# A decoder layer on one core: the mixing stage normalises one unit ahead, 18 of 48 expert tiles are turned in the projection, and the first branch weights are loaded before their stage

## What is computed

```python
h = rmsnorm(x, g_norm1) * (1.0 + scale1) + shift1
aq, ak, av, bb, bc, bx, cz, dq, dk, dv, gl = jnp.split(h @ w_in, SPLIT_POINTS, axis=-1)
ya = diff_attention(aq, ak, av, ...)                 # 4 heads, causal, softmax of two score maps each
yb = short_conv_mixer(bb, bc, bx, conv_w)
yc = multiscale_pool(cz, w_pool, pool_scale)
yd = sliding_window_sink_attention(dq, dk, dv, sinks) # 8 heads on 2 key heads, window of 128
branches = jnp.einsum('bsgc,gcd->bsgd', jnp.stack([ya, yb, yc, yd], axis=2), w_branch)
gates = jax.nn.sigmoid(gl.reshape(Bn, S, N_BRANCH, D_MODEL))
x = x + gate1 * (jnp.sum(gates * branches, axis=2) @ w_o)
return x + gate2 * peer_ffn(rmsnorm(x, g_norm2) * (1.0 + scale2) + shift2, ...)
```

## Time and profile before

| | us |
|---|---|
| median of 3 runs (lowest, highest) | 2081.24 (2071.46, 2083.84) |
| the profiled execution | 2083.53 |
| its span in the profile | 2081.7 |
| TensorE busy in the span | 1884.9 (91%) |
| VectorE, GpSimd, ScalarE busy | 1490.5, 770.8, 721.6 |

### The profile page before, as it was taken

The page is one execution under the profiler, slowest core; times in us unless marked ns, Lnnn a source line. Parts: engine busy times, 40 slices in busy tenths (PEclk is TensorE's granted clock), DMA queues, the critical chain, the costliest instruction groups (busy, mean ns, idle before and its releaser), DMA issues. The chain is left out here.

```text
span 2081.7 us, 28455 instructions
## 1 busy us (share of the span) xinstructions
PE 1884.9 (91%) x10096; PEld 1643.4 (79%) x10096; DVE 1490.5 (72%) x2260; ACT 721.6 (35%) x969; POOL 770.8 (37%) x487
## 2 busy tenths in 40 slices
PE   4999888889698989998999998999869999999998
PEld 4888666667486978888998988898858888888886
DVE  6444366665355658899987588878848888887887
ACT  3222233343324221323332354555533333333331
POOL 0000194000024000457877777787732332333320
PEclk7999989999799989999999999999989999999999
DMA  8754188888876051459999989999999999999991
GB/s 286 263 182 141 46 231 244 240 237 244 279 222 198 15 124 41 104 151 247 278 267 250 294 227 308 318 324 323 320 335 379 386 383 368 363 353 356 365 351 71
DMA packets 325795, 526.33 MB, mean 253 GB/s; under 512 B 20266, under 2 KB 243291, under 8 KB 321116
## 3 DMA queue, kind: packets, MB, share of 16 engines
q1 hardware_dynamic: 288860, 391.23, 61.6%
q0 software_dynamic: 36864, 134.23, 18.9%
HBM read 438.88 MB, written 85.99 MB: 252 GB/s over the span
## 5 line engine op out<-in xcount | busy, mean ns | idle before, releaser
L119 PE MATMUL u_s<-h_hi,u_hi 128*128 128x384 f32 x1024 | 359.2, 351 | 51.1 <-POOL u_lo L1775 46.4
L121 PE MATMUL u_s<-h_hi,u_lo 128*128 128x384 f32 x1024 | 350.0, 342 | 0.0
L120 PE MATMUL u_s<-h_lo,u_hi 128*128 128x384 f32 x1024 | 349.7, 342 | 0.0
L119 PE MATMUL v_o<-v_v_hi,v_w_hi 128*128 128x512 f32 x768 | 300.0, 391 | 19.1 <-DVE v_w_lo L1998 18.2
L120 PE MATMUL v_o<-v_v_lo,v_w_hi 128*128 128x512 f32 x768 | 299.6, 390 | 0.0
L121 PE MATMUL v_o<-v_v_hi,v_w_lo 128*128 128x512 f32 x768 | 299.5, 390 | 0.0
L119 PEld LDWEIGHTS u_s<-h_hi,u_hi 128*128 128x128 f32 x1024 | 197.9, 193 | 64.5 <-POOL u_lo L1775 38.0
L1937 ACT ACTIVATE v_v_hi<-v_raw 128x1024 fp32r<-128x1024 f32 x128 | 127.6, 1051 | 340.4 <-PE v_o L121 275.9
L1775 POOL TENSOR_TENSOR u_lo<-u_ut,u_hi 128x1024 fp32r<-128x1024 f32 x79 | 196.3, 2486 | 94.8 <-ACT u_hi L1553 94.4
L1964 DVE TENSOR_TENSOR v_v_lo<-v_raw,v_v_hi 128x1024 fp32r<-128x1024 f32 x128 | 149.4, 1220 | 92.7 <-ACT v_v_hi L1937 92.4
L120 PEld LDWEIGHTS u_s<-h_lo,u_hi 128*128 128x128 f32 x1024 | 198.0, 193 | 0.0
(11 more groups left out here) (310 smaller groups left out, 3879.1 us busy)
## 6 DMA issues: line engine op xcount, KB each, us to landing
v_raw<-in_v_experts_dram SPq DMA_DIRECT2D x128, 512.0 KB, 5.7
u_raw<-in_u_experts_dram SPq DMA_DIRECT2D x160, 256.0 KB, 6.3
gate_w_u_raw<-in_u_experts_dram SPq DMA_DIRECT2D x192, 128.0 KB, 4.0
turned_experts<-gate_w_u_t SPq DMA_DIRECT2D x48, 512.0 KB, 4.1
expert_acts<-u_ao SPq DMA_DIRECT2D x64, 384.0 KB, 5.3
u_raw<-turned_experts SPq DMA_DIRECT2D x96, 256.0 KB, 11.5
expert_gates<-u_gs SPq DMA_DIRECT2D x12, 2048.0 KB, 11.9
v_gt<-expert_gates SPq DMA_DIRECT2D x32, 768.0 KB, 14.4
```

Source lines behind the costliest of these rows:

```text
L119: nc.tensor.matmul(out, w[0], x[0], start=first, stop=False)
L120: nc.tensor.matmul(out, w[0], x[1], start=False, stop=False)
L121: return nc.tensor.matmul(out, w[1], x[0], start=False, stop=last)
```

## The change

Three things are done.

1. In `phase_mix` VectorE normalises unit n+1 in iteration n, after its scores were taken an iteration earlier, then turns rows, then does the split, then the scores of unit n+2. ScalarE does the exponentials of unit n+2 behind the split and ahead of the tanh. SyncE loads gate weights behind the turned rows and ahead of its wait for the tanh. In the last eight products the turn also stands ahead of the split.
2. 18 of the 48 tiles are turned in `phase_project`, between blocks 1 and 12, three in two blocks; the loops of SyncE, ScalarE and VectorE are written out there. The buffers lie where the results of blocks 13 to 16 go, so ScalarE waits for the turned tiles to be stored before it writes block 13. The other 30 are turned in the first 28 steps of `phase_mix` (`TURNING`), about one in each.
3. After step 28 of the mixing stage SyncE waits until all turned tiles are stored and loads the first two weight blocks of the gate stage into the two buffers of the turned tiles. The gate stage takes them from there, and its own buffers can take blocks 2 and 3 at once. VectorE waits for its second split before it writes over them.

```diff
-AHEAD = NE // P - PLAIN
+GATED = NE // P - PLAIN
+FRONT = 0
+AHEAD = GATED + FRONT
+IN_PROJECT = 18
+IN_MIX = AHEAD - IN_PROJECT
...
+def turned_tile(n):
+    return PLAIN + n if n < GATED else n - GATED
...
+FIRST_TURN, LAST_TURN = 1, 12
+def projected_by(b):
+    return IN_PROJECT * max(0, min(LAST_TURN, b) + 1 - FIRST_TURN) // (LAST_TURN + 1 - FIRST_TURN)
...
+            rows_in(0)
+            rows_in(1)
+            for b in range(4, NB):
+                i, j = b // 4, b % 4
                 sp.wait_ge(lo_ok, b - 3)
                 sp.dma_start(raw[j][:, :, :], cols(b)).then_inc(w_in[j], 16)
-            with sp.Fori(1, NB // 4) as i:
-                for j in range(4):
-                    load(4 * i + j, j)
-                    if j >= 2:
-                        sp.wait_ge(share_ok, 16 * i + 8 * (j - 1) - 16)
-                        sp.dma_start(ring[j - 2][:, :, :], ada[:, :, bass.ds((4 + 2 * i + j - 2) * S, S)]).then_inc(ada_in[j - 2], 16)
-            load(NB - 1, 0)
+                if i < 4 and j >= 2:
+                    sp.wait_ge(share_ok, 16 * i + 8 * (j - 1) - 16)
+                    sp.dma_start(ring[j - 2][:, :, :], ada[:, :, (4 + 2 * i + j - 2) * S:(5 + 2 * i + j - 2) * S]).then_inc(ada_in[j - 2], 16)
+                for t in range(projected_by(b - 4), projected_by(b - 3)):
+                    sp.wait_ge(u_turned, t + 1)
+                    sp.dma_start(turned_slot(turned, t), u_t[t % 2][:, :, :].rearrange("p m e -> p (m e)")).then_inc(u_out[t % 2], 16)
+                    if t + 2 < IN_PROJECT:
+                        rows_in(t + 2)
+            for j in range(2):
+                sp.wait_ge(u_out[j], 16 * (IN_PROJECT // 2))
...
+                if b == LAST_TURN + 1:
+                    act.wait_ge(u_turned, IN_PROJECT)
+                    for x in range(2):
+                        act.wait_ge(u_out[x], 16 * (IN_PROJECT // 2))
...
+            def turn_rows(b):
+                for t in range(projected_by(b - 1), projected_by(b)):
+                    j = t % 2
+                    dve.wait_ge(u_in[j], 64 * (t // 2) + 64)
+                    if t >= 2:
+                        dve.wait_ge(u_out[j], 16 * (t // 2))
+                    turn_tile(nc, u_t[j], u_raw[j]).then_inc(u_turned, 1)
...
+                turn_rows(4 * i)
                 split_lo(4 * i + 2, 2)
                 shares(i, range(5, 11))
+                turn_rows(4 * i + 1)
                 split_lo(4 * i + 3, 3)
                 shares(i, range(11, 16))
+                turn_rows(4 * i + 2)
...
+TURNING = 28
 def turned_by(n):
-    return AHEAD * (n + 1) // (NBR * KD)
-def phase_mix(nc, a, keep, xt, y_hi, y_lo, tanhs, turned):
+    return IN_MIX * min(n + 1, TURNING) // TURNING
...
+            sp.wait_ge(sem["g_lo"], 1)
+            load(2)
             for n in range(NG):
-                if n + 2 < NG:
-                    sp.wait_ge(sem["g_lo"], n + 1)
-                    load(n + 2)
                 for t in range(turned_by(n - 1), turned_by(n)):
                     sp.wait_ge(sem["u_turned"], t + 1)
-                    sp.dma_start(turned[t // 2, :, t % 2 * D:(t % 2 + 1) * D], u_t[t % 2][:, :, :].rearrange("p m e -> p (m e)")).then_inc(sem[f"u_out{t % 2}"], 16)
-                    if t + 2 < AHEAD:
+                    sp.dma_start(turned_slot(turned, IN_PROJECT + t), u_t[t % 2][:, :, :].rearrange("p m e -> p (m e)")).then_inc(sem[f"u_out{t % 2}"], 16)
+                    if t + 2 < IN_MIX:
                         rows_in(t + 2)
+                if n + 3 < NG:
+                    sp.wait_ge(sem["g_lo"], n + 2)
+                    load(n + 3)
+                if n == TURNING:
+                    for j in range(2):
+                        sp.wait_ge(sem[f"u_out{j}"], 16 * (IN_MIX // 2))
+                        load_branch(sp, a, b_first[j], 1, j).then_inc(first_in[j], 16)
                 sp.wait_ge(sem["th_ok"], n + 1)
                 sp.dma_start(tanhs[n], th[n % 2][:, :]).then_inc(sem[f"th_out{n % 2}"], 16)
...
             exps(0)
+            exps(1)
             for n, (kind, i, h) in enumerate(units):
-                if n + 1 < NU:
-                    exps(n + 1)
                 act.wait_ge(sem["tr"], n + 1)
                 if n >= 2:
                     act.wait_ge(sem["pv"], n - 1)
                 nb = len(blocks(n))
                 nc.scalar.activation(pt[:, n % 2, 0:nb, :], p_t[:, 0:nb, :], ACT.Copy).then_inc(sem["pt_ok"], 1)
                 split_hi(n + 1)
+                if n + 2 < NU:
+                    exps(n + 2)
                 tanh(n)
...
             scores_in(0)
             split_lo(0)
+            scores_in(1)
+            normalise(0)
             for n in range(NU):
                 if n + 1 < NU:
-                    scores_in(n + 1)
-                normalise(n)
+                    normalise(n + 1)
+                turn_rows(n)
                 split_lo(n + 1)
-                turn_rows(n)
+                if n + 2 < NU:
+                    scores_in(n + 2)
...
+def load_branch(eng, a, to, g, d):
+    wb = a["w_branch"][0].rearrange("g (k p) n -> p (g k) n", p=P)
+    return eng.dma_start(to[:, :, :], wb[:, CB * g:CB * g + CB, d * BW:(d + 1) * BW])
...
+                if not isinstance(r, int) or r:
                     sp.wait_ge(sem["lo_ok"], s - 1)
-                sp.dma_start(raw[j][:, :, :], wb[:, bass.ds(4 * g, CB), d * BW:(d + 1) * BW]).then_inc(sem[f"b_in{j}"], 16)
+                if not isinstance(r, int) or r or d >= 2:
+                    sp.dma_start(raw[j][:, :, :], wb[:, bass.ds(4 * g, CB), d * BW:(d + 1) * BW]).then_inc(sem[f"b_in{j}"], 16)
...
+                first = isinstance(r, int) and s < 2
+                if first:
+                    act.wait_ge(first_in[j], 16)
+                else:
+                    act.wait_ge(sem[f"b_in{j}"], (2 * r + d // 2) * 16)
                 if wait:
                     act.wait_ge(sem["mm"], 2 * s - 2)
-                nc.scalar.activation(hi[j][:, :, :], raw[j][:, :, :], ACT.Copy).then_inc(sem["hi_ok"], 1)
+                nc.scalar.activation(hi[j][:, :, :], (b_first if first else raw)[j][:, :, :], ACT.Copy).then_inc(sem["hi_ok"], 1)
...
+                    if first and d == 1:
+                        dve.wait_ge(sem["lo_ok"], 2)
```

More of the change, by code:

```diff
@@ L456, in _ @@
             turn(0, True)
-            with dve.Fori(1, NB // 4) as i:
+            for i in range(1, NB // 4):
                 turn(i)
@@ L2078, in program @@
         tanhs = nc.dram_tensor("gate_tanhs", [NBR * KD, P, S], F32, kind="Internal").ap()
[L2079 to L2080 removed]
+        kb = Kit(nc, top, "branch", Y_AT + 56 * KB)
+        b_first, first_in = [kb.sb(f"first{j}", [P, CB, BW]) for j in range(2)], [kb.sem(f"first_in{j}") for j in range(2)]
+        phase_mix(nc, a, keep, xt, *(y[:, :, :].rearrange("p (g c) t -> p g c t", c=CB) for y in (y_hi, y_lo)), tanhs, turned, b_first, first_in)
         if stop <= 3:
```

68 lines of the change are left out of this document (36 added, 32 removed).

## The result

The changed kernel takes 2025.56 us (median of 4 runs, 2024.32 to 2035.27), the kernel before 2081.7 us beside it (4 runs, 2071.46 to 2083.84). The ratio is 0.9746, 95% interval 0.9707 to 0.9785. The forecast was 2036 us, range 2018 to 2056. The profiled execution took 2025.17 us, with a span of 2023.3.

What follows compares the result with a forecast made beforehand. The prediction took the mixing stage to be held by an order of hand-overs, no engine but TensorE being full. Its terms, -31 - 8.3 - 8.6 + 3 = -45 us, took the median 2081.2 to 2036 us, range 2018 to 2056.

Steps and rivals of the forecast that it cites:

- The units, -31: Mixing stage's 24 attention units: normalising one unit ahead removes waits for normalised scores; 202 us, 31 us less.
- The 9 us for GpSimd's company: First ten attention units: GpSimd working beside VectorE lengthens the loop by 0.9 us each, 9 us.
- the thin place: ScalarE's queue in the units: tanh behind the next exponentials, expected done some 1.5 us before TensorE needs it.
- The eight products, -8.3: Last eight gate products of the mixing stage: earlier weight requests, no turns after unit 27; 58.8 becomes 50.5 us.
- The gap, -8.6: Before the first branch product: last tanh store issued earlier and weights already loaded, so it starts 8.6 us earlier.
- The projection, +3: First 13 projection blocks: 18 added turns bring transfers near their limit; cost between 0 and 11 us, 3 taken.
- After 570 us, nothing: Rest of the kernel: the change touches only the gate stage's first loads there, so no saving was counted.
- B: Rival: VectorE, ScalarE and GpSimd's lock-outs make the loop bind; units 216 us, total 2050; chance 0.14.
- C: Rival: TensorE hardly waits; units 191 us, tail 49, nothing lost in the projection, total 2020; chance 0.12.
- D: Rival: in the units the wait only moves to the tanh; tail and gap alone gain, total 2067; chance 0.05.
- A: The forecast case itself, all terms as summed: 2036 us (2027 to 2047); chance 0.65.
- E: Rival: turns in the projection pace its blocks through transfers, 15.6 us instead of 10.9 each; total 2090; chance 0.04.

Runs made afterwards that it cites:

- the repeats: Two more groups of runs of the changed kernel with nothing edited: medians 2028.46 and 2029.85 us.
- light_pool: The changed kernel with GpSimd leaving out the pooling's adds and two of three convolution taps, so the output differs: 2022.35 us.
- late_pool: The changed kernel with GpSimd's pooling and convolution held back until unit 11 has ended: 2031.33 us.
- tanh_first: The changed kernel with ScalarE taking the tanh of product n before the exponentials of unit n+2: 2025.31 us.
- after_again: The changed kernel run once more with nothing edited: 2028.46 us, ratio 0.9766 to the kernel before.
- all_in_mix: The changed kernel with no tiles turned in the projection, all 48 in the mixing stage by unit 27: 2056.87 us.
- old_order: The changed kernel with VectorE's and ScalarE's steps in the order of the kernel before, the other parts kept: 2045.31 us.
- turn_24: The changed kernel with 24 tiles turned in the projection instead of 18, and 24 in the mixing stage: 2034.69 us.
- z_split: The changed kernel with GpSimd's 128x2048 product of the convolution's inputs issued as four of 128x512: 2026.93 us.
- after: The changed kernel itself, as first measured and profiled: 2025.56 us, ratio 0.9746 to the kernel before.

## Why the prediction was right

**The units, -31.** Measured -31.7, and -30.2 and -29.7 by the repeats. The waits for normalised scores went whole (39.0 to 7.0: the 32 I took). TensorE's busy time fell by 10.6 us, where I took 8 for the clock. That this is close is in part luck: I had matmuls in 16 of the 28 us at 1.2 GHz and let all of those go, while they were in 27.7 and 17.4 of these went, and the clock explains 8.7 us, not all of the 10.6. The 9 us for GpSimd's company came as 10.7 us of waits for the tanh, 8.6 of it at products 3 and 9 and not spread over ten units; the two small waits come behind 390 us, where GpSimd is silent. That GpSimd's company is the cause light_pool and late_pool confirm; its price in late_pool, 11.3 us, is near the 9. The step behind it, that the tanh queued behind the exponentials is the thin place, holds: tanh_first takes the waits away. In the wide units, where loop and cycle had come out equal, TensorE hardly waits: it is busy 113.93 of the last 116.10 us (after_again, above).

**The eight products, -8.3.** Measured -8.6. The number was right and its reason only in part. I put it down to the weights' earlier request and to turns that end with unit 27. all_in_mix has both and takes 57.4 us, 1.1 less than the kernel before. The rest came with the lower number of tiles (five turned in these products and not seven, at a share of 0.67 and not 0.81 for the transfers), which I counted for the loop of the units alone; old_order, with the same five tiles and the old order, takes 51.1.

**The gap, -8.6.** Measured -9.9. The issue of the last store, 0.8 us after the transposes began, and the 2.37 us from the split to TensorE came as I said. Mis-sized were the store's landing (2.46 us, not 3.48) and the 0.3 us from there to the split (0.03). The prediction cites the Trainium skill (DMA: Bandwidth & Descriptors, Anatomy of one DMA) for a fixed cost of about 2.0 us. That section is on transfers that GpSimd issues, and this store is SyncE's; no run here splits its 2.46 us.

**The projection, +3.** Measured 0: TensorE was busy 141.66 of 141.90 us. The sum of demand (144 to 153 us of transfers in 142) was about right, a share of 0.98, but I charged a wait where the last transfers simply ran on beside blocks that turn nothing. How near the edge it is, turn_24 shows: 7 us for six tiles more.

**After 570 us, nothing.** The profile after had 8.2 us less there, 7.3 of it in the gathered phase. The prediction rightly gave the change nothing; what it lacked was the spread of that phase, 18 us over fourteen profiles, one per cent of the span less a little. With it the error resolves: the parts up to the first branch product sum to -50.2 us, where -45 was forecast (3 from the projection, 1.3 from the gap, 0.7 from the units, 0.3 from the products). The rest of the 56 us between the two first medians fits the scatter: the later medians are 50.8 and 49.8 us apart.

**The rivals and the signs.** B needed units of 216 us, C 191, D 233: none came. The first median, 2025.56 us, nevertheless lies between A's own band (2027 to 2047) and C's 2020; the later two, 2028.46 and 2029.85, lie in A's. Two of C's terms did come, nothing lost in the projection and a tail of 49 to 50 us. Its third, that TensorE hardly waits, is met by tanh_first at 195 us, not by the change. B's and D's mechanism, a wait that moves to the tanh, is there in small with 30 tiles (10.7 us) and in full with 48 (29.0 us in all_in_mix). E is a real mechanism at 36 tiles, 1% slower than before. Two of the signs failed without harm to the argument: the clock in the units was 0.96, not 0.97 or more, and the gap was 5.7 us as the prediction measures it (5.3 in the table), not 6 to 8.

The Trainium skill (SBUF — State Buffer, Who interferes with whom) says that whichever of the two engines issues first holds the shared access for its whole instruction and the other blocks. The trace agrees to 0.01 us, 4.51 and 4.52 us, and z_split agrees with the whole-instruction part of it, 1.19 us once the pieces are short. The page also names TENSOR_SCALAR, in its two-port modes, beside instructions with two inputs. The row of 1.12 us in z_split, 0.17 us in the row of after, fits that, though no row shows in which mode it ran.

## What to carry to other kernels

When a wait sits between two engines that hand work back and forth, look for the step that one of them could take a unit earlier, and then ask which step now stands behind the early one in the other engine's queue: here a 0.6 us tanh behind exponentials that waited. Work moved to a stage with idle transfers was free here only until that stage's own transfers were full: 18 tiles cost nothing, 24 cost 7 us, 36 cost 75. When two versions are compared for what their order is worth, count first how much work each has inside the stage. When a term is small beside the scatter of a phase that the change never touches, judge it by stage times, not by the end-to-end median.

## What the runs showed that was not expected

- A VectorE instruction on 128x4 elements took 4.52 us beside a GpSimd instruction of 4.51 us, and 0.16 us in z_split. The block is no idle time in the profile: it is counted as busy.
- Putting off 70 us of GpSimd's work by 100 us moved its cost of 11 to 12 us and did not lower it. Moving one tanh on ScalarE took more than half of it away.
- A phase whose transfers' share is 0.95 took 686 to 704 us in fourteen profiles; its rows shown above give 188 to 189 MB each. In the three profiles of the changed kernel each stage ahead of it repeated within 2 us.
